# Context queries and keys kept on chip, and five reorderings, in a two-layer mixer step on one core

## The chip, the cores and the metric

The kernel is one program on one core of a Trainium2 chip. Its engines are TensorE (PE: matrix products and, through products with an identity, transposes), VectorE (DVE), ScalarE (ACT), GpSimd (POOL) and SyncE (SP, which here only issues DMAs). Each runs its own list of instructions in order, and they meet through semaphores. The metric is the time of one execution on the device in microseconds (us); lower is better.

## The reference

256 context tokens (`prompt`) and 1024 latent tokens (`sample`), each of 1024 numbers, pass two layers, all in float32.

```python
h = rmsnorm(x, norm1) * (1 + sc1) + sh1            # sc1, sh1: columns of silu(cond) @ w_mod + b_mod
# layer 0
proj = h @ w_in                                    # c_q 384 | c_kv 256 | k_rope 32 | gate_b, gate_c, u: 512 each
q = rmsnorm(rmsnorm(c_q) @ w_q_up)                 # 8 heads of 96
k, v = mla_expand_kv(rmsnorm(c_kv), k_rope)        # 8 heads of 96 and 64
# latent tokens: q and k rotated; cached context keys (256) go ahead of their own keys (1024)
attn = softmax(q k / sqrt(96)) v                   # context tokens see context tokens only
conv = gate_b * short_conv(gate_c * u)             # 3 taps along the tokens, each group by itself
x = x + g1 * (concat(attn, conv) @ w_o)
# layer 1 mixes by a 2-D DFT and a linear map instead
# both layers end with 16 experts; each takes its best 32 context and 128 latent tokens
ye = (silu(xe @ w_gate) * (xe @ w_up)) @ w_down * g
x = x + g2 * zeros.at[idx].add(ye)
```

## The kernel before, in words

The work is cut into stages; each stage (`Stage`) has its own tiles and semaphores and ends with a barrier of all engines. In order: `projections`, `attention`, `output_and_choice` (tiles `mix`), `experts` of layer 0, `fourier_and_choice`, `experts` of layer 1. The token axis is cut into ten tiles of 128: tiles 0 and 1 are the context, tiles 2 to 9 the latent tokens. Two more tiles hold the cached context, of which only keys and values are made.

**Projections.** Before the tiles come the modulation vectors: eight products of `cond` with 1 MB loads of `w_mod` (`mod.step`, L216), added to the bias by DVE (L232), turned to columns by PE (L224) and used by DVE to scale and shift the normalised, transposed tile (L706, L709). SP issues the eight `w_mod` loads (four staging buffers, so that loads 4 to 7 wait for products 0 to 3), then the first columns of `w_in`, then the four small loads of the bias (L192), then the other weights. POOL issues the tiles of `x` (L459). PE then goes through each tile: latents (`latent_product`, L507), u part (L514), transposes of the previous tile's queries and keys (`query_turns`, `key_turns`, L491), transposes of this tile's latents (L483), c part (L514), query and key/value products (L539, L548), transposes of the tile after next (L469), b part (L514). Tiles 3 and 5 also make the values of the cached tiles in between the two halves of the b part, and the tile after each (4 and 6) turns the cached keys (`k_c`) right behind its own. DVE copies turned keys from PSUM to `k_out` (`keys_kept`, L728), of which there is one buffer, and SP stores it to HBM (`kt`); `q_out` goes to `qt` likewise. For the convolution DVE writes `gated` = gate_c x u, applies three taps into `conv_o` (L747, L751), multiplies by gate_b (L755), and SP stores each half to `conv`.

**Attention.** SP loads the context's queries and keys from `qt` and `kt` (L905, L906), then values, the first latent queries, and ten pieces of the latent tokens' keys (L916). PE works through 72 slots (one head of one tile, for the context one head of both tiles): scores (L965 context, L980 latent), transposes, values. The output weights `w_o` are loaded during the last tile's slots into a tile `room` that outlives the stage.

**Output (`mix`).** SP loads attention and convolution rows of the first tile (`mixed(0)`, L1400 and L1401), and PE multiplies them by `w_o` (L1462).

**Experts.** POOL gathers token rows by index and, behind each expert, adds its result to rows of HBM by a DMA that accumulates: `scatter_sample` (L1722, 128 rows) and `scatter_prompt` (L1729, 32 rows). A scatter waits for the landing of the one before it of its own kind, since rows may repeat. The context results of experts 12 to 15 come in one product, so four context scatters stand at the end.

Of the kernel before, what the change touches and what calls it, by code (L numbers as in the profile page):

```python
# [32 lines left out]
P = 128  # L33
# [227 lines left out]
def projections(nc, t, per):  # L261
# [10 lines left out]
    PAD = 1  # L272
    WIDTH = TOK + 4 * PAD
    with Stage(nc, "proj") as s:
# [23 lines left out]
        gated = s.sb("gated", [P, CJ, WIDTH])  # L298
# [11 lines left out]
        gated_flat = gated[:].rearrange("p j n -> p (j n)")  # L310
        w_mod = [gated_flat[:, 0:2 * D], gated_flat[:, 2 * D:4 * D], gate_b[:].rearrange("p a j n -> p (a j n)"),
                 h_t[1][:].rearrange("p k n -> p (k n)")]
# [27 lines left out]
        for n in range(NT):  # L340
            count(lp_uses, ("lat", n))
            if n == 0:
                count(tp_uses, ("x", 1))
            else:
                count(tp_uses, ("q", n - 1))
                count(tp_uses, ("k", n - 1))
            if n - 1 in CACHED_AT:
                count(tp_uses, ("k", NT + CACHED_AT[n - 1]))
            count(tp_uses, ("lat", n))
# [14 lines left out]

        def at(p):

            return PAD + p * PAIR + (2 * PAD if p else 0)

# [9 lines left out]
        with nc.Block() as block:  # L378

            @block.sync  # L380
            def _(sp):
# [10 lines left out]
                mod.load_bias(sp, 0)  # L392
# [22 lines left out]
                def queries_store(n):  # L415
                    for b in range(2):
# [3 lines left out]
                def keys_store(n):  # L420
                    for b in range(2):
# [3 lines left out]
                def conv_store(p, half):  # L425
                    sp.wait_ge(mixed, mix_uses[p, half] + 1)
                    j = slice(half * JH, (half + 1) * JH)
                    sp.dma_start(t["conv"].rearrange("j p n -> p j n")[:, j, p * PAIR:(p + 1) * PAIR], conv_o[:, j, :]).then_inc(conv_out[half], 16)
# [22 lines left out]
                for done, value in ((q_stored, 16 * NT), (k_stored, 16 * KEYT), (v_stored, 16 * KEYT), (lat_stored, 32 * PT),  # L451
# [4 lines left out]
            def _(pool):  # L456
                for n in range(NT):
# [4 lines left out]
            def _(pe):  # L462
# [102 lines left out]
                for n in range(NT):  # L565
# [10 lines left out]
                    if n - 1 in CACHED_AT:  # L576
                        key_turns(NT + CACHED_AT[n - 1])
# [3 lines left out]
                    if n < LAST:  # L581
                        c_part(n)
                    if n == 0:
# [20 lines left out]
            def _(act):  # L604
# [42 lines left out]
                def queries_kept(n):  # L647
                    wait(act, q_stored, 16 * n)
# [1896 lines left out]
```

## Time and profile before

| | |
|---|---|
| median of 3 runs | 2297.88 us (2296.34 to 2303.9) |
| profiled execution | 2297.82 us, of which the span of the profile is 2295.4 us |
| mean granted TensorE clock | 0.939 of full speed |
| PE busy | 89% of the span |
| DVE, ACT, POOL busy | 38%, 20%, 7% |
| HBM traffic | 403.98 MB, mean 176 GB/s |

All times in what follows are us from the start of the span. A timeline row gives the start, the duration of a run of equal instructions, the engine, the line, output<-inputs, the count, and in brackets how long the engine had been idle before and what ended that. "Idle before" is what a change can win back, and only on the engine that sets the end of its stage; in most stages that is PE.

### The profile page before, as it was taken

The page shows a single profiled execution, that of the slowest core. Times are in us where ns is not written, and L with a number is a line of the kernel's source. Part 1 is how long each engine was busy: PE and PEld are TensorE (multiplying, and loading weights), DVE is VectorE, ACT ScalarE, POOL GpSimd, SP SyncE. Part 2 cuts the span into 40 slices and gives each one's busy share as a digit, 9 for nine tenths or more (in the row PEclk, how much of TensorE's full clock was granted, in tenths as well). Part 3 has the DMA queues.
Part 4 walks back from the last instruction along what each step waited for, and adds up shares of the span by engine and source line. Part 5 has one row for each costly group of instructions (what it writes and reads, how often), then busy time and mean ns, then how long its engine had stood idle before and what let it go on. Part 6 is the DMA issues. An engine that isn't in the chain of part 4 may idle for free. (4 is left out here: it accounts for less than half of the span.)

```text
span 2295.4 us, 27522 instructions
## 1 busy us (share of the span) xinstructions
PE 2038.8 (89%) x11435; PEld 1433.3 (62%) x11435; DVE 862.9 (38%) x1791; ACT 469.3 (20%) x922; POOL 154.4 (7%) x134
## 2 busy tenths in 40 slices
PE   4999989959999998992999999976997199999996
PEld 2777767745666664441878787851443187878784
DVE  1354345345666563337222222215254722222221
ACT  1222222126665662111000000004122100000000
POOL 0000000000000000000011121111010001211111
PEclk8999999979999999995899999986998599999998
DMA  9211110058444224952568787816020766878771
GB/s 356 84 46 37 53 35 33 24 131 264 178 164 182 106 84 144 368 189 98 194 225 310 264 305 267 288 28 235 19 110 37 291 238 226 307 266 302 266 258 28
DMA packets 160981, 403.98 MB, mean 176 GB/s; under 512 B 12357, under 2 KB 31740, under 8 KB 154714
## 3 DMA queue, kind: packets, MB, share of 16 engines
q1 hardware_dynamic: 145322, 347.18, 42.2%
q0 software_dynamic: 15536, 55.06, 8.7%
q8 instruction: 90, 1.47, 0.3%
q14 instruction: 33, 0.27, 0.0%
HBM read 338.65 MB, written 63.55 MB: 175 GB/s over the span
## 5 line engine op out<-in xcount | busy, mean ns | idle before, releaser
L1776 PE MATMUL experts_gu<-experts_h_t,weights_w_gate 128*128 128x160 f32 x2048 | 303.7, 302 | 4.1 <-issue 4.1
L1776 PEld LDWEIGHTS experts_gu<-experts_h_t,weights_w_gate 128*128 128x128 f32 x2048 | 289.7, 192 | 19.2 <-issue 19.2
L1776 PE MATMUL experts_gu<-experts_h_t,weights_w_up 128*128 128x160 f32 x2048 | 300.2, 300 | 0.0
L1776 PEld LDWEIGHTS experts_gu<-experts_h_t,weights_w_up 128*128 128x128 f32 x2048 | 286.5, 191 | 0.0
L1800 PE MATMUL experts_dn<-weights_w_down,experts_hid 128*128 128x512 f32 x512 | 225.8, 594 | 0.0
L1841 DVE TENSOR_TENSOR experts_hid<-experts_act,experts_gu 128x160 f32<-128x160 f32 x128 | 41.1, 321 | 481.3 <-ACT experts_act L1830 481.3
L514 PE MATMUL proj_cv<-proj_h_t,proj_w_in 128*128 128x256 f32 x960 | 216.0, 384 | 2.6 <-DVE proj_h_t L709 2.6
L1830 ACT ACTIVATE experts_act<-experts_gu 128x160 f32<-128x160 f32 x128 | 38.8, 303 | 834.1 <-PE experts_gu L1776 834.1
L514 PEld LDWEIGHTS proj_cv<-proj_h_t,proj_w_in 128*128 128x128 f32 x960 | 184.0, 193 | 29.9 <-issue 4.7
L1800 PEld LDWEIGHTS experts_dn<-weights_w_down,experts_hid 128*128 128x128 f32 x512 | 94.8, 190 | 113.8 <-issue 113.8
L980 PE MATMUL attn_sc<-attn_keys_s,attn_q_s 96*128 96x512 f32 (+1 forms) x384 | 154.9, 539 | 3.8 <-DVE attn_pr_t L1113 2.7
L1462 PE MATMUL mix_acc<-layer_room,weights_w_down 128*128 128x512 f32 x320 | 144.2, 603 | 9.3 <-DMA weights_w_down<-conv 9.3
L1095 DVE TENSOR_REDUCE attn_least<-attn_sc 128x1 f32<-128x512 f32 (+1 forms) x192 | 109.6, 599 | 102.1 <-PE attn_sc L980 102.1
L980 PEld LDWEIGHTS attn_sc<-attn_keys_s,attn_q_s 96*128 96x128 f32 x384 | 67.8, 190 | 91.3 <-issue 63.9
L1046 ACT ACTIVATE attn_pr<-attn_sc,attn_neg 128x1280 f32<-128x1280 f32 x64 | 85.0, 1327 | 128.3 <-DVE attn_neg L1097 128.3
L1462 PEld LDWEIGHTS mix_acc<-layer_room,weights_w_down 128*128 128x128 f32 x320 | 59.8, 193 | 78.8 <-issue 76.2
L1053 ACT ACTIVATE attn_pr<-attn_pr,attn_inv 128x512 f32<-128x512 f32 (+2 forms) x144 | 106.3, 785 | 3.9 <-DVE attn_inv L1103 3.9
L507 PE MATMUL proj_lp<-proj_w_in,proj_h_t 128*128 128x384 f32 (+1 forms) x320 | 93.7, 452 | 3.3 <-DVE proj_h_t L709 3.3
L2097 PE MATMUL mix_banks<-weights_w_down,weights_w_up 128*128 128x512 f32 (+2 forms) x96 | 58.5, 749 | 32.8 <-DMA weights_w_down<-w_f_folded 32.8
L1113 DVE COPY attn_pr_t<-attn_sc 128x512 f32<-128x512 f32 x128 | 82.5, 686 | 1.7 <-PE attn_sc L994 1.7
L507 PEld LDWEIGHTS proj_lp<-proj_w_in,proj_h_t 128*128 128x128 f32 x320 | 61.5, 193 | 33.5 <-issue 5.2
L994 PE MATMUL attn_sc<-all_ident,attn_pr 128*128 128x128 f32 x640 | 80.7, 273 | 0.1
(357 smaller groups left out, 2066.4 us busy)
## 6 DMA issues: line engine op xcount, KB each, us to landing
weights_w_gate<-w_gate_l SPq DMA_DIRECT2D x32, 2048.0 KB, 9.5
weights_w_up<-w_up_l SPq DMA_DIRECT2D x32, 2048.0 KB, 17.2
weights_w_down<-w_down_l SPq DMA_DIRECT2D x32, 2048.0 KB, 16.4
attn_w_mod<-w_mod_l SPq DMA_DIRECT2D x40, 1024.0 KB, 5.1
proj_w_in<-w_in_l SPq DMA_DIRECT2D x3, 2048.0 KB, 19.2
proj_x<-x POOLq DMA_DIRECT2D x10, 512.0 KB, 3.9
weights_w_down<-x SPq DMA_DIRECT2D x10, 512.0 KB, 5.1
kt<-proj_k_out SPq DMA_DIRECT2D x12, 384.0 KB, 3.0
```

What stands on the lines that cost most here:

```text
L507: last = pe.matmul(lp[:, base:base + hi - lo], h_t[n // 2 % 2][:, k, cols], w_in[:, k, lo:hi], start=(k == 0), stop=(k == KD - 1))
L514: last = pe.matmul(cv[bank][:, j * PAIR:(j + 1) * PAIR], w_in[:, k, base + j * P:base + (j + 1) * P], h_t[p % 2][:, k, :], start=(k == 0), ...
L980: pe.matmul(sc[b][:, lo:hi], q_s[tile % 2][:, h * P:(h + 1) * P], keys_s[:, h, lo:hi], start=True, stop=True).then_inc(s_full, 1)
L994: last = pe.transpose(sc[b][:, m * P:(m + 1) * P], pr[b][:, m * P:(m + 1) * P], per.ident[:])
L1046: act.activation(pr[b][:], sc[b][:, 0:K], ACT.Exp, bias=neg[b][:, 0:1], scale=-1.0, accum_out=total[b][:, 0:1]).then_inc(p_ready, 1)
L1053: act.activation(pr[b][:, lo:hi], pr[b][:, lo:hi], ACT.Copy, scale=inv[b][:, a:a + 1]).then_inc(p_scaled, 1)
L1095: ch.add(dve.tensor_reduce(least[:, k:k + 1], sc[b][:, lo:hi], AX.X, ALU.min))
L1113: dve.tensor_copy(pr_t[n % 4][:, lo:hi], sc[n % 2][:, lo:hi]).then_inc(v_kept, 1)
L1462: last = pe.matmul(acc[u][:, half * BANK:(half + 1) * BANK], a_t[u][:, k, :], w_o[:, k, half * BANK:(half + 1) * BANK], start=(k == 0), st ...
L1776: last = pe.matmul(gu[j % 2][:, m * SLOTS:(m + 1) * SLOTS], w[u][:, k, j * P:(j + 1) * P], h_t[u][:, k, :], start=(k == 0), stop=(k == KD ...
L1800: last = pe.matmul(dn[half][:], hid[i][:, k, 0:CAP_S], wd[i][:, k, cols], start=(k == 0), stop=(k == KF - 1))
L2097: last = pe.matmul(out[0:dst.shape[0], cols], stationary, moving, start=(m == 0), stop=(m == len(terms) - 1))
```

## The change

Seven pieces, in the order of the program:

1. The four bias loads go from SP's queue to the head of POOL's, ahead of the tiles of `x`. The `w_mod` staging moves to other buffers (two of them in `room_a`).
2. PE turns the cached keys after the c part of tiles 4 and 6, and the cached latents ahead of the b part of tiles 3 and 5; DVE and ACT are reordered to match.
3. `gated` is kept per pair of tiles, with the two columns at its edges copied, and the last taps write to the region of `conv_o` whose store is older.
4. Queries and keys of tiles 0 and 1 are written into `room_a` (`room.q_p`, `room.keys_p`) and read there by the attention: four stores to and four loads from HBM vanish, with PE's waits for them.
5. The first `mixed` rows are loaded during the last slots of the attention (`load_first`); `w_o` is loaded in two halves.
6. At the end of each layer the last latent scatter is issued between the second and third of the four context scatters.
7. One more stage (`rest0`) holds what follows the projections in layer 0: one more barrier at the layer's end.

```diff
@@ projections, SP's list
                 sp.dma_start(w_in[:, :, 0:LAT], w_in_d[:, :, 0:LAT]).then_inc(w_lat_in, 16)
-                mod.load_bias(sp, 0)
@@ POOL's list
             def _(pool):
+                mod.load_bias(pool, 0)
                 for n in range(NT):
@@ PE's list
                         key_turns(n - 1)
-                    if n - 1 in CACHED_AT:
-                        key_turns(NT + CACHED_AT[n - 1])
                     latent_turns(n)
...
                     if n < LAST:
                         c_part(n)
+                    if n - 1 in CACHED_AT:
+                        key_turns(NT + CACHED_AT[n - 1])
...
                     if n in CACHED_AT:
+                        latent_turns(NT + CACHED_AT[n])
                         b_part(n, 0, 1)
-                        latent_turns(NT + CACHED_AT[n])
                         kv_up(NT + CACHED_AT[n])
@@ ACT's queries_kept
+                    dst = room.q_p[0:QK, n, :] if n < PT else q_out[:]
@@ DVE's keys_kept
+                        if n < PT:
+                            dst, src = room.keys_p[0:QK, 4 * b:4 * b + 4, n * P:(n + 1) * P], tp[b][0:QK, :].rearrange("c (h k) -> c h k", h=4)
@@ DVE's gate
+                    if p >= 2:
+                        ch.add(dve.tensor_copy(here[:, :, 0:1], before[:, :, PAIR:PAIR + 1]))
+                        ch.add(dve.tensor_copy(before[:, :, PAIR + 1:PAIR + 2], here[:, :, 1:2]))
+                    if p == PAIRS - 1:
+                        ch.add(dve.memset(here[:, :, PAIR + 1:PAIR + 2], 0.0))
+                    ch.settle()
+                def taps(p, half):
+                    use, out, src = mix_uses[p, half], region(p, half), gated[:, p % 2, half * JH:(half + 1) * JH, :]
+                    wait(dve, conv_out[use % 2], 16 * (use // 2))
...
                 def convolve(p, half):
-                    lo = at(p)
                     dve.wait_ge(b_kept, 2 * p + half + 1)
-                    wait(dve, conv_out[half], 16 * p)
...
@@ DVE's list
-                    if n - 1 in CACHED_AT:
-                        keys_kept(NT + CACHED_AT[n - 1])
                     if n < LAST:
                         gate(n)
                         if n >= 2:
+                            taps(n // 2 - 1, n % 2)
                             convolve(n // 2 - 1, n % 2)
...
+                    if n - 1 in CACHED_AT:
+                        keys_kept(NT + CACHED_AT[n - 1])
                     query_sums(n)
@@ attention
-                for n in range(PT):
-                    sp.dma_start(q_p[:, n, :], t["qt"][n * QK:(n + 1) * QK, :]).then_inc(qp_in, 16)
-                    sp.dma_start(keys_p[:, :, n * P:(n + 1) * P], t["kt"][n * QK:(n + 1) * QK, :].rearrange("c (h k) -> c h k", h=HEADS)).then_inc(kp_in, 16)
                 sp.dma_start(vals_p[:], t["v"][0:SEQ, :].rearrange("(m p) c -> p m c", p=P)).then_inc(vp_in, 16)
...
                     if n == SLOTS_N - HEADS:
                         room.load_output_weights(sp, t)
+                        sp.wait_ge(o_out[0], 48)
+                        room.load_first(sp, t)
...
-                        if n == 0:
-                            pe.wait_ge(qp_in, 16 * PT)
-                            pe.wait_ge(kp_in, 16 * PT)
@@ output_and_choice
-                mixed(0)
                 choice.load(sp)
...
                pe.wait_ge(room.w_o_in, 32)
+                pe.wait_ge(room.first_in, 32)
                 product(0, 0, 0, KD)
@@ experts, POOL's list
                     if e == NE - 1:
                         for m in range(NE - BATCH, NE):
+                            if m == NE - 2:
+                                scatter_sample(e)
                             scatter_prompt(m)
...
```

PE's list around tile 3's b part and the whole of tile 4 up to its query products is, in the kernel before (`lat_c`, `k_c` are the cached tile's latents and keys, `xh` the tile after next, `cv` the c, b and u parts):

```order
L469 MATMUL proj_tp<-all_ident,proj_xh 128x128 x8
L514 MATMUL proj_cv<-proj_h_t,proj_w_in 128x256 x8
L483 MATMUL proj_tp<-all_ident,proj_lat_c 128x128 x2
L548 MATMUL proj_lp<-proj_w_kv,proj_lat_t 128x512 x4
L514 MATMUL proj_cv<-proj_h_t,proj_w_in 128x256 x8
L507 MATMUL proj_lp<-proj_w_in,proj_h_t 128x384 x8
L507 MATMUL proj_lp<-proj_w_in,proj_h_t 128x288 x8
L514 MATMUL proj_cv<-proj_h_t,proj_w_in 128x256 x16
L491 MATMUL proj_tp<-all_ident,proj_q_n 96x128 x8
L491 MATMUL proj_tp<-all_ident,proj_k_n 96x128 x8
L491 MATMUL proj_tp<-all_ident,proj_k_c 96x128 x8
L483 MATMUL proj_tp<-all_ident,proj_lat 128x128 x5
```

And the same stretch of PE's list in the changed kernel (its line numbers are a few lower):

```order
L466 MATMUL proj_tp<-all_ident,proj_xh 128x128 x8
L480 MATMUL proj_tp<-all_ident,proj_lat_c 128x128 x2
L511 MATMUL proj_cv<-proj_h_t,proj_w_in 128x256 x8
L545 MATMUL proj_lp<-proj_w_kv,proj_lat_t 128x512 x4
L511 MATMUL proj_cv<-proj_h_t,proj_w_in 128x256 x8
L488 MATMUL proj_tp<-all_ident,proj_q_n 96x128 x8
L488 MATMUL proj_tp<-all_ident,proj_k_n 96x128 x8
L480 MATMUL proj_tp<-all_ident,proj_lat 128x128 x5
L511 MATMUL proj_cv<-proj_h_t,proj_w_in 128x256 x16
L488 MATMUL proj_tp<-all_ident,proj_k_c 96x128 x8
```

The cached latents moved from behind the first half of the b part to ahead of it, and the cached keys from directly behind the tile's own keys to behind the tile's c part.

POOL's list ends, in the kernel before (L1717 gathers, L1722 is the latent scatter, L1729 the context scatter), with:

```order
L1722 DMA y_sample<-experts_ys,all_at_s 1024x1024
L1717 DMA experts_xs<-xh_sample,all_at_s 128x1024
L1729 DMA y_prompt<-experts_yp,all_at_p 256x1024
L1722 DMA y_sample<-experts_ys,all_at_s 1024x1024
L1729 DMA y_prompt<-experts_yp,all_at_p 256x1024 x4
L1722 DMA y_sample<-experts_ys,all_at_s 1024x1024
```

and in the changed kernel with:

```order
L1759 DMA y_sample<-experts_ys,all_at_s 1024x1024
L1766 DMA y_prompt<-experts_yp,all_at_p 256x1024
L1759 DMA y_sample<-experts_ys,all_at_s 1024x1024
L1766 DMA y_prompt<-experts_yp,all_at_p 256x1024 x2
L1759 DMA y_sample<-experts_ys,all_at_s 1024x1024
L1766 DMA y_prompt<-experts_yp,all_at_p 256x1024 x2
```

Of the four context scatters two now stand behind the last latent scatter; layer 0 ends with the same rows on its own tensors.

## Rows read from the trace of the kernel before

**Rows 1.** Waits of PE by line and releaser: total us, times, longest.
```profile
PE proj_tp L483 <- DVE proj_k_out L728: 10.1, 9, 3.4
...
PE proj_lp L548 <- ACT proj_lat_t L623: 2.3, 2, 1.2
```

**Rows 2.** Timeline of all engines, 0 to 60 us.
```profile
3.57 1.32 POOL L459 DMA_DIRECT2D proj_x<-x  x2 [3.12 <-POOLq L2440]
...
7.66 1.06 ACT L610 ACTIVATE proj_junk<-proj_x 128x1024 f32<-128x1024 f32 x1 [0.26 <-DMA proj_x<-x]
...
11.46 1.97 PE L469 MATMUL proj_tp<-all_ident,proj_xh 128*128 128x128 f32 x8 [4.28 <-DVE proj_xh L699]
...
15.27 1.19 SPq L181 DMA_DIRECT2D proj_gated<-w_mod_l  x2
...
21.98 5.06 SPq L192 DMA_DIRECT2D proj_mod_bias<-b_mod_l  x4
...
37.29 0.69 DVE L232 TENSOR_TENSOR proj_mod_rows<-proj_up,proj_mod_bias 128x512 f32<-128x512 f32 x1 [15.85 <-DMA proj_mod_bias<-b_mod_l]
...
42.49 10.89 PE L507 MATMUL proj_lp<-proj_w_in,proj_h_t 128*128 128x384 f32 x32 [3.34 <-DVE proj_h_t L709]
```

**Rows 3.** Tile proj_x, 2 to 70 us: issue to landing.
```profile
DMA to landing us min/median/max: 4.0/7.3/8.1
```

**Rows 4.** Windows: length, busy by engine, PE clock, DMA share, GB/s.
```profile
6.00:36.00 30.00, 13.68 (x75) 2.98 (x75) 1.27 (x4) 4.36 (x8) 0.53 (x1) 0.82 1.02 419
```

**Rows 5.** Windows of one tile each: tile 2, tile 4, tile 6.
```profile
127.85:169.45 41.60, 40.70 (x178) 31.05 (x177) 18.55 (x41) 9.22 (x22) 0.53 (x1) 1.00 0.14 45
...
216.10:263.78 47.68, 43.54 (x187) 33.02 (x185) 19.50 (x40) 9.40 (x23) 0.53 (x1) 0.96 0.15 47
...
310.43:359.27 48.84, 44.22 (x186) 33.72 (x185) 19.48 (x40) 9.41 (x23) 0.00 (x0) 0.93 0.11 36
```

**Rows 6.** Timeline of all engines, tile 4.
```profile
235.04 1.15 PE L491 MATMUL proj_tp<-all_ident,proj_k_c 128*96 128x128 f32 x8 [0.50 <-DVE proj_k_out L728]
...
238.59 1.28 DVE L728 COPY proj_k_out<-proj_tp 96x512 f32<-96x512 f32 x2 [3.10 <-DMA kt<-proj_k_out]
```

**Rows 7.** Timeline of all engines, 484 to 500 us.
```profile
486.17 0.61 DVE L747 TENSOR_SCALAR proj_conv_o<-proj_gated,proj_conv_w 128x256 f32<-128x256 f32 x2 [2.25 <-DMA conv<-proj_conv_o]
...
494.94 0.32 SPq L905 DMA_DIRECT2D attn_q_p<-qt  x1
```

**Rows 8.** Timeline of PE, 500 to 545 us.
```profile
504.93 3.75 PE L965 MATMUL attn_sc<-attn_keys_p,attn_q_p 96*128 96x256 f32 x8 [19.19 <-DMA attn_keys_p<-kt]
...
533.29 2.67 PE L980 MATMUL attn_sc<-attn_keys_s,attn_q_s 96*128 96x512 f32 x6
```

**Rows 9.** Tile attn_keys_s: its loads (duration ns min/median/max, first and last start) and landing.
```profile
L916 SPq DMA_DIRECT2D attn_keys_s<-kt x10: 562/1622/4797, 498.5 to 517.4; - x10
...
DMA to landing us min/median/max: 7.6/8.3/12.5
```

**Rows 10.** Windows: the start of the attention.
```profile
489.50:520.00 30.50, 11.71 (x34) 8.00 (x36) 7.66 (x16) 7.97 (x23) 0.00 (x0) 0.50 0.96 208
```

**Rows 11.** Timeline of all engines, 870 to 890 us.
```profile
877.53 0.33 SPq L1400 DMA_DIRECT2D weights_w_down<-attn  x1
...
881.38 9.11 PE L1462 MATMUL mix_acc<-layer_room,weights_w_down 128*128 128x512 f32 x16 [7.61 <-DMA weights_w_down<-conv]
```

**Rows 12.** Timeline of all engines, 2262 to 2296 us.
```profile
2274.72 0.75 DVE L1875 SCALAR_TENSOR_TENSOR experts_ys<-experts_dn,all_g_s,experts_gate 128x512 f32<-128x512 f32 x1 [2.68 <-PE experts_dn L1800]
2277.29 1.32 POOL L1729 DMA_INDIRECT y_prompt<-experts_yp,all_at_p  x1 [3.02 <-DMA y_prompt<-experts_yp,all_at_p]
...
2283.23 1.55 POOL L1722 DMA_INDIRECT y_sample<-experts_ys,all_at_s  x1 [0.30 <-issue]
```

**Rows 13.** Windows: the last data of the span.
```profile
2288.00:2290.00 2.00, 0.00 (x0) 0.00 (x0) 0.00 (x0) 0.00 (x0) 0.00 (x0) 0.50 0.27 51
```

**Rows 14.** Waits of SP, 1540 to 1560 us: the three barriers at the end of layer 0.
```profile
SPq L133 <- PEq L133: 1.1, 3, 0.5
```

More of the change, by code:

```diff
@@ L271, in projections @@
     LAST = NT - 1
-    PAD = 1
-    WIDTH = TOK + 4 * PAD
     with Stage(nc, "proj") as s:
@@ L450, in _ @@
                 keys_store(LAST)
-                for done, value in ((q_stored, 16 * NT), (k_stored, 16 * KEYT), (v_stored, 16 * KEYT), (lat_stored, 32 * PT),
+                for done, value in ((q_stored, 16 * (NT - PT)), (k_stored, 16 * (KEYT - PT)), (v_stored, 16 * KEYT), (lat_stored, 32 * PT),
                                     (conv_out[0], 16 * PAIRS), (conv_out[1], 16 * PAIRS)):
@@ L739, in gate, with region @@
                     dve.wait_ge(c_kept, n + 1)
+                    if p >= 2:
[4 more added lines that the diff above has]
+                    ch.settle()
+                def region(p, half):
+                    return conv_o[:, (mix_uses[p, half] % 2) * JH:(mix_uses[p, half] % 2 + 1) * JH, :]
@@ L754, in convolve @@
-                    j = slice(half * JH, (half + 1) * JH)
-                    dve.tensor_tensor(conv_o[:, j, :], conv_o[:, j, :], gate_b[:, p % 2, j, :], ALU.mult).then_inc(mixed, 1)
+                    dve.tensor_tensor(region(p, half), region(p, half), gate_b[:, p % 2, half * JH:(half + 1) * JH, :], ALU.mult).then_inc(mixed, 1)
                 def sums(sq, ready_in, value, out, ready):
@@ L1462, in product @@
                         last = pe.matmul(acc[u][:, half * BANK:(half + 1) * BANK], a_t[u][:, k, :],
-                                         w_o[:, k, half * BANK:(half + 1) * BANK], start=(k == 0), stop=(k == KD - 1))
+                                         room.row(k)[:, half * BANK:(half + 1) * BANK], start=(k == 0), stop=(k == KD - 1))
                     if half == 1 and hi == KD:
@@ L1643, in experts @@
     with Stage(nc, f"experts{layer}") as s:
-        gate = room.room[:, 0:2, :] if room else s.sb("gate", [P, 2, D])
-        xs = [room.room[:, 6 + u, :] if room else s.sb(f"xs{u}", [P, D]) for u in range(2)]
-        xp = room.room[:, 5, :] if room else s.sb("xp", [P, D])
+        gate = room.parts[0][:, 0:2, :] if room else s.sb("gate", [P, 2, D])
+        xs = [room.row(6 + u) if room else s.sb(f"xs{u}", [P, D]) for u in range(2)]
+        xp = room.row(5) if room else s.sb("xp", [P, D])
         h_t = [s.sb(f"h_t{u}", [P, KD, SLOTS]) for u in range(2)]
@@ L1650, in experts @@
         hid = [s.sb(f"hid{b}", [P, KF, SLOTS]) for b in range(BATCH)]
-        ys = [room.room[:, 2 + u, :] if room else s.sb(f"ys{u}", [P, D]) for u in range(2)]
-        yp = room.room[:, 4, :] if room else s.sb("yp", [P, D])
+        ys = [room.row(2 + u) if room else s.sb(f"ys{u}", [P, D]) for u in range(2)]
+        yp = room.row(4) if room else s.sb("yp", [P, D])
         tp = [s.ps(f"tp{b}") for b in range(2)]
```

127 lines of the change are left out of this document (77 added, 50 removed).

## The prediction

> **What bounds the kernel now.** The page's busy shares come first: PE has 89% of the span, DVE 38%, the others less, so a change pays where PE stands idle, or at a stage's end where all engines wait for a transfer. The waits of PE, sorted by releaser, give the map. The one that reaches most places is that of the latents' transposes for a copy by DVE, nine times, longest 3.4 us [rows 1]. The timelines then show what each wait is for. At the start DVE idles 15.85 us for the bias and PE begins the first latents at 42.49 [rows 2]. A tile of the projections takes 41.60 us when nothing special happens, and 47.68 and 48.84 where cached keys are turned [rows 5]. The attention begins with 19.19 us of PE waiting for keys that this kernel itself stored [rows 8], the output stage with 7.61 us for its first rows [rows 11], and each layer ends with scatters behind an idle PE [rows 12]. The experts, the bulk of the span, are not touched except for that end.
>
> All sums are made against the profiled execution, 2297.82 us (2.4 us of it outside the span), which is within 0.1 us of the median of the three runs.
>
> **1. Bias on POOL's queue: 1.5 us (bounds -1.2 and 5.4).** The bias is issued at 21.98 behind everything that SP sent before it, and DVE uses it at 37.29; PE's first latents follow 5.2 us later [rows 2]. With the bias early, DVE could go on when PE's last modulation product is done, and the first latents wait for the first columns of `w_in`. From 6 to 36 us the DMA engines are full (share 1.02, 419 GB/s) [rows 4], and everything up to those columns is in that stretch, so they land at about 36 to 37. Were nothing else moved, PE could begin at about 37.1: a gain of 5.4.
>
> But POOL issues the tiles of `x` behind the bias now. Two `x` issues take 1.32 us, so four bias issues take 2.6; DVE must have zeroed the bias tile first, for which I allow 0.8. So `x` is issued at 3.57 + 3.4 = 7.0, when SP's loads are already in the queues. The first tile landed 4.1 us after its issue (7.66 less 3.57), later ones take 7.3 [rows 2, 3]. It then lands at 14.3 in place of 7.66, 6.6 later, and PE's transposes move from 11.46 to 18.1. PE's list has these ahead of the modulation products, and loads 4 to 7 wait for the products to free their buffers: the first goes from 15.27 to about 21.9. By then the first four have landed, the queues run empty, and 4 x 1.05 MB and 2.75 MB of `w_in` (1024 x 672 numbers) remain, 16.6 us at 419 GB/s, with some 2.5 us from an issue to data (4.1 less the 1.25 that half a megabyte takes). That is 41.0 in place of 42.49: 1.5. With SP's price for a bias issue (5.06 for four) and the longest landing, 8.1, `x` comes 3.3 us later still and the gain is about -1.2; both stay in the range.
>
> The Trainium skill ("DMA: Bandwidth & Descriptors", section "Issuing engines are not separate DMA queues") says that transfers started by different engines run on the same 16 DMA engines and interleave, and that issuing from several saves only the issue time. By that rule this piece gives nothing, and the total would be 1.5 us higher; the full DMA engines of [rows 4] agree with it, no run here has yet shown the order in which the bias would land.
>
> **2. Cached tiles: 10.5 us (8.0 to 11.5).** In tile 4 PE turns the cached keys at 235.04; DVE cannot copy them out before the store of the tile's own keys has landed, since there is one `k_out`: it waits 3.10 us for that DMA and copies from 238.59 [rows 6]; PE's next transposes need the same PSUM and wait for that copy [rows 1]. Behind the wait PE's clock also falls: the mean granted clock is 0.96 and 0.93 in tiles 4 and 6, and 1.00 in tile 2 [rows 5]. The change puts the c part between the two, 32 products of 128x256, which at the least take four times the 1.15 us of the eight small ones [rows 6], so the store (issued when the copy of the tile's own keys ends) has landed before the cached keys are turned. The tile then takes that of an ordinary one plus the turn itself, 1.15 less the overlap of about 0.15: 42.6. That is 5.1 and 6.2 us for the two. What is late next is DVE's copy of the cached keys (1.28), which must be done before the transposes of the tile after next need the PSUM; the query and value products in between hide it. Without that cover it costs 1.28 in each tile.
>
> The cached latents lose a little: they stand right behind the transposes of another tile, whose PSUM DVE frees by two multiplications with an addition between (0.69 each for 128x512, as in DVE's row of [rows 2]), 2.07 less the 0.5 that the first half is done earlier, so some 1.6 us of waiting twice. The waits for the copies that they replace are 2.3 us in two [rows 1]. Net -0.8, no more than -0.9. So 11.3 less 0.8; the lower bound adds the two uncovered copies.
>
> **3. Last taps: 1.85 us (0.2 to 2.25).** DVE waits 2.25 us for a store of `conv_o` before the last taps [rows 7], and the copy of the last keys, whose store ends the stage, is queued behind. The other region's store is long done. Of that go the edge copies, on DVE in the last `gate`: three operations that the trace doesn't have. From below they cost nothing, since DVE waits for PE there; from above three times 0.69 [rows 2]. They write one or two columns, so I take 0.4. In the other tiles DVE, with its low share, hides them.
>
> **4. Context queries and keys: 9.7 us (5.8 to 13).** The stage's first DMA is at 494.94 [rows 7], PE begins at 504.93 [rows 8]. With the operands in place it begins when it is through the barrier, some 0.3 after SP: 495.2, so 9.7 earlier. What is late next are the latent keys: PE first reads them at 533.29, 28.4 after its beginning [rows 8], which becomes 523.6 on the old scale. Their last load is issued at 517.4 and lands 8.3 later, at 525.7 [rows 9]: a slack of 7.6. Four loads of 393 KB go from ahead of them; the DMA engines are full there (share 0.96 at 208 GB/s) [rows 10], so 1.57 MB make them 7.5 us earlier. Slack 7.6 + 7.5 - 9.7 = 5.4; with the longest landing, 12.5, still 1.2. If they come earlier only by SP's four issues (two thirds of the 3.6 between 494.94 and 498.5, 2.4 [rows 7, 9]) and take 12.5, PE waits 3.9: the lower bound 5.8. PE's clock is 0.50 in this stretch, with 11.71 us of products [rows 10]; if it rises some 6 us of products sooner, 3 more: the upper bound. The context's copies to the new places are as long as the old ones, on the same engines.
>
> **5. First rows of the output stage: 3.65 us (3.0 to 3.85).** SP is through the barrier at 877.53, PE begins at 881.38 [rows 11]. With the rows loaded one tile earlier, PE begins some 0.2 behind SP: 3.65. The loads are issued during the last tile's 8 slots, tens of us ahead, and wait only for stores of tiles done long before. The second tile's rows move up in SP's list by two issues and have a whole tile's product to land under.
>
> **6. Last scatters: 2.5 us in each layer, 5.0 (3.5 to 7).** Context scatters go out 4.3 us apart, since each waits for the one before (2277.29; the next ends 0.30 before 2283.23, so it began at 2281.60) [rows 12]. The latent scatter stands last, is ready when DVE ends at 2275.47, but is issued at 2283.23; data flows until about 2288.6 (a share of 0.27 in the last window) [rows 13]. Now it goes out at 2275.75 and takes POOL 1.55 us, to 2277.3, so the third context scatter starts at 2277.6, 0.3 late, and the fourth at 2281.9. That lands about 3.6 after its start (4.3 less the 0.7 until the next issue), at 2285.5; 0.5 MB of latent rows flow beside the third and may delay it by up to 1. The end moves from 2288.6 to 2285.5 to 2286.5: 2.1 to 3.1, I take 2.5, bounds 1.75 and 3.5. Layer 0 has the same list, and nothing of the next stage starts before the barrier, so twice.
>
> **7. One more barrier: -0.6 us (-0.4 to -2.3).** Three stand at the end of layer 0 already, with 1.1 us of waits in all [rows 14]; a fourth costs a third of that and some clearing, 0.6. At most: from the last data at 2288.6 to the end of the span, 2295.4, three stage ends take 6.8, so 2.3 for one.
>
> **Sum.** 1.5 + 10.5 + 1.85 + 9.7 + 3.65 + 5.0 - 0.6 = 31.6 us; 2297.82 - 31.6 = 2266.2, so 2266. All lower bounds together give 17.0 (2280.8), all upper 42.6 (2255.2).
>
> **The rivals.**
> - *The start gives nothing or loses* (the rule named above, or slow bias issues): the sum is 30.1 or 28.9, so 2267.7 to 2268.9. For it: `x` does queue behind the bias, and the DMA engines are full [rows 4]. Against: the first latents now wait for a bias that is last of all. 0.15.
> - *The latent keys become the bound of the attention's start.* Piece 4 falls to 5.8 at worst: 2270. For it: the slack rests on 1.57 MB fewer bytes ahead. Against: 5.4 us of slack by medians. 0.08.
> - *Tiles 4 and 6 find another wait*: DVE's new order (edge copies, taps, then the cached keys) is late for the next transposes and costs as much as the old wait in both, 2 x 3.2, so 2272.6. Against: DVE is 19.5 of 47.68 us busy in that tile [rows 5]. 0.08.
> - *PE's clock is better than before* in the attention's start: 2262 to 2255. 0.10.
> - *The change moves waits rather than removing them*: half of pieces 2, 4 and 5 comes back, 12 us, 2278. 0.05.
> - *Slower than before.* PE's clock stays at its lower level far into the attention, because PE works there from the start in short bursts between DVE and ACT. At the level of 0.50 [rows 10] products take twice as long, so each us there loses half a us: 63 us more at that level eat the 31.6, from 77 on the kernel is slower by more than 0.3%, and 90 would give 2311. Against: PE's gaps between the bursts are as long as before. 0.02, and 0.02 that the pieces cancel to no change.
>
> **How the numbers follow.** The forecast itself, 2261 to 2271 with the start at its middle value, has 0.50; the first rivals lie within 2267 to 2273. The range 2254 to 2280 reaches both sums of bounds. 0.3% of this kernel, 6.9 us, is about what a measurement can tell from no change; only the last rivals come near it. So faster 0.95, no change 0.03, slower 0.02.
>
> **What would show it.** First latents at about 41.0, bias ended long before DVE adds it; tiles 4 and 6 at 42.6 with a clock of 1.00 and no wait of DVE for a store of keys; no wait of PE at the attention's beginning, latent keys landed when PE comes to them; PE's first output product 0.2 us behind the barrier; the last context scatter at about 4.3 us behind the third, and 2.5 us less to the end of each layer. The prediction is wrong if the DMA engines at the start are idle longer than the bias saves, if the latent keys are waited for, or if DVE's new order shows up as waits of PE in every tile.

## The result: 28.5 us less, and where they came from

The changed kernel takes 2269.17 us (median of 4 runs, 2268.7 to 2275.16), the kernel before 2297.65 (median of 4): ratio 0.9877, 95% interval 0.9852 to 0.9901. Forecast were 2266 and a range of 2254 to 2280. The profiled execution took 2269.41 us, 2267.0 of it the span, 28.4 less than the span before.

A span hides which piece did what, so the two traces were cut at the same instructions. "First latents" is the start of the first latent product, "tile 0" from there to the next, "tiles 1 to 8" to the last latent product, "last tile" on to DVE's first zeroing in the attention, "attention" on to DVE's first in the output stage, "output" on to POOL's first gather, "experts 0" on to the first of the last four context scatters, "end 0" on to layer 1's first transfer by POOL, "layer 1" on to the first of its last four context scatters, "end 1" to the end of the span. All in us:

| stage | before | changed | difference | forecast of the pieces in it |
|---|---|---|---|---|
| first latents | 42.49 | 43.03 | +0.5 | -1.5 |
| tile 0 | 43.84 | 45.93 | +2.1 | 0 |
| tiles 1 to 8 | 355.27 | 344.32 | -10.95 | -10.5 |
| last tile | 53.52 | 51.47 | -2.05 | -1.85 |
| attention | 382.48 | 373.27 | -9.2 | -9.7 |
| output | 204.73 | 200.49 | -4.2 | -3.65 |
| experts 0 | 445.64 | 444.68 | -1.0 | 0 |
| end 0 | 27.06 | 25.13 | -1.9 | -2.5 + 0.6 |
| layer 1 | 713.68 | 714.72 | +1.0 | 0 |
| end 1 | 26.69 | 23.96 | -2.7 | -2.5 |

The timeline of the changed kernel's start, all engines, shows the piece that went the other way:

```profile
4.63 2.29 POOL L192 DMA_DIRECT2D proj_mod_bias<-b_mod_l  x4 [4.18 <-DVE proj_mod_bias L205]
...
6.92 1.09 POOL L456 DMA_DIRECT2D proj_x<-x  x2
15.91 1.06 ACT L607 ACTIVATE proj_junk<-proj_x 128x1024 f32<-128x1024 f32 x1 [9.65 <-DMA proj_x<-x]
...
19.71 1.97 PE L466 MATMUL proj_tp<-all_ident,proj_xh 128*128 128x128 f32 x8 [13.67 <-DVE proj_xh L698]
...
23.55 0.33 SPq L181 DMA_DIRECT2D proj_gate_b<-w_mod_l  x1
...
37.76 0.69 DVE L232 TENSOR_TENSOR proj_mod_rows<-proj_up,proj_mod_bias 128x512 f32<-128x512 f32 x1 [11.27 <-PE proj_up L216]
...
41.66 0.69 DVE L708 TENSOR_TENSOR proj_h_t<-proj_h_t,all_shift 128x512 f32<-128x512 f32 x1
...
43.03 11.43 PE L504 MATMUL proj_lp<-proj_w_in,proj_h_t 128*128 128x384 f32 x32 [3.87 <-DMA proj_w_in<-w_in_l]
```

`x` is issued at 6.92 and lands at 15.9, 9.0 us later, where the first tile took 4.1 before [rows 2]. Everything that hangs on it moves: PE's transposes to 19.71, the fifth weight load to 23.55. DVE no longer waits for the bias, but adds it at 37.76, no sooner than before, since the products are late; and PE now waits for `w_in` instead. That wait is last by only 0.7 us: DVE, late with the products, ends the scaled tile at 42.35 (41.66 and 0.69), as in the kernel before (42.34). So an earlier `w_in` alone would have given no more than that.

The windows of tiles 4 and 6 of the changed kernel (length, busy by engine, PE clock, DMA share, GB/s) answer to [rows 5]:

```profile
218.96:261.44 42.48, 41.58 (x187) 31.86 (x185) 19.26 (x42) 9.41 (x23) 0.53 (x1) 1.00 0.16 53
308.48:350.95 42.47, 41.57 (x186) 31.86 (x185) 19.26 (x42) 9.40 (x23) 0.00 (x0) 1.00 0.13 41
```

Both have the clock at 1.00 and 42.5 us. PE's timeline around the first of them shows why, and what tile 3 pays:

```profile
207.21 0.30 PE L480 MATMUL proj_tp<-all_ident,proj_lat_c 128*128 128x128 f32 x1 [0.44 <-DVE proj_h_t L705]
208.45 0.33 PE L480 MATMUL proj_tp<-all_ident,proj_lat_c 128*128 128x128 f32 x1 [0.94 <-DVE proj_h_t L705]
...
245.48 1.04 PE L488 MATMUL proj_tp<-all_ident,proj_k_c 128*96 128x128 f32 x8
```

The cached keys are turned without a wait; the cached latents wait twice for DVE, 1.4 us in all, where in the kernel before the key and value product behind them waited 1.16 for ACT's copy [rows 1].

DVE's timeline at the end of the last tile has the last taps without the wait of [rows 7]:

```profile
475.82 0.61 DVE L760 TENSOR_SCALAR proj_conv_o<-proj_gated,proj_conv_w 128x256 f32<-128x256 f32 x2
```

PE's timeline at the attention's beginning, for [rows 8]:

```profile
484.60 3.75 PE L980 MATMUL attn_sc<-layer_room_a 96*128 96x256 f32 x8 [7.18 <-PEq L133]
...
512.98 3.40 PE L995 MATMUL attn_sc<-attn_keys_s,attn_q_s 96*128 96x512 f32 x6
```

PE starts 0.04 us behind SP's first DMA (484.56), not 9.99. The latent keys, issued and landed by the view of their tile as

```profile
L932 SPq DMA_DIRECT2D attn_keys_s<-kt x10: 636/1510/2353, 485.5 to 498.2; - x10
...
DMA to landing us min/median/max: 6.2/7.9/8.6
```

are there at 506.8 at the latest, 6 us before PE reads them at 512.98.

One row each of DVE's and PE's timelines at the output stage's beginning, and POOL's timeline at the end of layer 1, answer to [rows 11, 12]:

```profile
858.02 0.06 DVE L1582 MEMSET mix_eps<- 128x1 f32 x1 [6.28 <-PEq L133]
...
858.14 6.16 PE L1498 MATMUL mix_acc<-layer_room_a,rest_first 128*128 128x512 f32 x8 [3.94 <-PEq L133]
```

```profile
2247.30 1.32 POOL L1766 DMA_INDIRECT y_prompt<-experts_yp,all_at_p  x1 [2.94 <-DMA y_prompt<-experts_yp,all_at_p]
2250.07 1.55 POOL L1759 DMA_INDIRECT y_sample<-experts_ys,all_at_s  x1 [1.46 <-DVE experts_ys L1915]
2251.93 1.32 POOL L1766 DMA_INDIRECT y_prompt<-experts_yp,all_at_p  x1 [0.30 <-issue]
2257.42 1.31 POOL L1766 DMA_INDIRECT y_prompt<-experts_yp,all_at_p  x1 [4.17 <-DMA y_prompt<-experts_yp,all_at_p]
```

PE begins 0.12 us behind DVE. The third context scatter starts 0.3 late, as forecast, and the fourth 5.49 behind it in place of 4.31.

### The profile page after: what moved, and what is told of

Read it like the earlier page. It is cut to its first block and busy times, and to the rows that moved or that the text cites. A ratio compares the mean times of both kernels' runs of the same rounds, so it can differ in the third digit from the quotient of the medians.

```text
span 2267.0 us, 27538 instructions
## 1 busy us (share of the span) xinstructions
PE 2036.6 (90%) x11435; PEld 1431.2 (63%) x11435; DVE 864.4 (38%) x1804; ACT 469.5 (21%) x922; POOL 155.8 (7%) x138
## 5 line engine op out<-in xcount | busy, mean ns | idle before, releaser
L1009 PEld LDWEIGHTS attn_sc<-all_ident,attn_pr 128*128 128x128 f32 x640 | 74.0, 141 | 6.8 <-ACT attn_pr L1068 0.5
L1030 PE MATMUL attn_o<-attn_pr_t,attn_vals_s 128*64 128x128 f32 x1280 | 76.9, 275 | 0.6 <-DVE attn_pr_t L1128 0.6
```

The lines of the kernel that those rows point to most:

```text
L1009: last = pe.transpose(sc[b][:, m * P:(m + 1) * P], pr[b][:, m * P:(m + 1) * P], per.ident[:])
L1030: last = pe.matmul(o_ps[VH * side:VH * (side + 1), base:base + width], vals[:, m, h * VH:(h + 1) * VH], pr_t[n % 4][:, m * width:(m + 1) * ...
```

## The experiments

Twelve runs. Five are the changed kernel with one piece undone (the bias, the cached tiles, the attention's operands, the first rows, the last scatters), three move one of its edits to another place, two put several such edits together, and two repeat the changed kernel and the kernel before. Pieces 3 and 7 have no run that undoes them alone. One execution of each was profiled; spans differ by several us in stages that no edit touches (layer 1 alone took 710.9 to 717.1 in the fourteen profiles), so each piece is priced in its own stage.

**The start.** Three places for the bias:

```diff
@@ bias_behind: back on SP
             def _(pool):
-                mod.load_bias(pool, 0)
...
                 sp.dma_start(w_in[:, :, 0:LAT], w_in_d[:, :, 0:LAT]).then_inc(w_lat_in, 16)
+                mod.load_bias(sp, 0)
@@ x_then_bias: on POOL behind two tiles of x
-                mod.load_bias(pool, 0)
                 for n in range(NT):
+                    if n == 2:
+                        mod.load_bias(pool, 0)
                     wait(pool, x_ready, n - 1)
@@ bias_head_sp: on SP ahead of the weights
-                mod.load_bias(pool, 0)
...
+                mod.load_bias(sp, 0)
                 for n in range(4):
                     mod.load(sp, n)
```

> The changed kernel with the bias loads back on SP behind the first columns of w_in; all else as changed. Theory 1 (x is late because it queues behind the bias and beside the weights): the first tile of x lands at about 7.7 us in place of 15.9, the first latents start at 42.5 in place of 43.0, tile 1's latents at 86.4 in place of 88.96, and the span is 2.6 us shorter, 2264.4. Theory 2 (the start is set by the bytes that must come before the first latents, and the place of the bias does not matter): first latents at 43.0, tile 1 at 89.0, span 2267.

Measured: 2267.41 us (4 runs, 0.9874 of before, 0.9854 to 0.9894). First latents at 42.71, near the 42.5 of theory 1, but tile 1's at 88.31, not 86.4: tile 0 still took 45.6. So the place of the bias does not explain tile 0. As to the start, 42.71 lies below the seven profiles with the bias in the changed kernel's place (42.75 to 44.52) by too little to decide; the next run does.

> The changed kernel with the bias on POOL's queue behind the first two tiles of x instead of ahead of them. Theory 1 (x late): x lands at about 7.7, PE's first transposes start at 11.5 in place of 19.7, the weight loads 4 to 7 start at 15.3 in place of 23.6, DVE adds the bias at about 31.5, the first columns of w_in land at about 36.5 and the first latents start at about 36.8; 6 us less at that point, of which the other weights of tile 0 may keep some: span 2259 to 2263. Theory 2 (bytes set the start): first latents at 42 to 43, span 2266 to 2267.

Measured: 2261.66 us (4 runs, 0.9843 of before, 0.9824 to 0.9862), first latents at 36.98. Its timeline, all engines (the rows to set beside the changed kernel's above):

```profile
4.78 2.03 POOL L192 DMA_DIRECT2D proj_mod_bias<-b_mod_l  x4
...
7.51 1.06 ACT L608 ACTIVATE proj_junk<-proj_x 128x1024 f32<-128x1024 f32 x1 [0.42 <-DMA proj_x<-x]
...
11.31 1.97 PE L467 MATMUL proj_tp<-all_ident,proj_xh 128*128 128x128 f32 x8 [4.43 <-DVE proj_xh L699]
...
31.17 0.69 DVE L232 TENSOR_TENSOR proj_mod_rows<-proj_up,proj_mod_bias 128x512 f32<-128x512 f32 x1 [9.68 <-PE proj_up L216]
```

The same four loads, one row lower in POOL's list: `x` lands at 7.5, DVE adds the bias 6.6 us earlier than in the changed kernel, and only `w_in` is waited for (PE 4.41 us). Theory 2 fell. Of the 6.05 us at the first latents 5.07 are left at tile 1's (83.89), since tile 0 took 46.9.

> The changed kernel with the bias ahead of the weight loads on SP's queue, so that POOL starts with x. Theory 1 (x late): x lands by about 9, PE's first transposes start at about 12 to 13; the weights start one bias later (2.3 to 5 us), and the first latents at 38 to 41. Theory 2 (bytes set the start): 42 to 43. Theory 3 (an early bias itself is what delays whatever follows it, on any queue): the weights are late by 8 as x was, first latents after 44.

Measured: 2262.28 us, first latents at 38.24, `x` landed by 7.92, the four bias issues 1.14 us at the head of SP's list. Theory 1 again. The first latents are 1.26 us later than with the bias behind `x`, about the 1.14 us of issues: an early bias by itself costs little more than its issues.

**The cached tiles.** Both moves undone on PE, ACT and DVE (`key_turns` and `keys_kept` of the cached tile back behind the tile's own, `latent_turns` back behind `b_part(n, 0, 1)`, `latents_kept` behind `key_root`).

> The changed kernel with the cached keys and latents at their old places on PE, ACT and DVE; all else as changed. Theory 1 (the one buffer k_out and its store made the wait, and the clock fell behind it): tiles 4 and 6 take 47.7 and 48.8 us again in place of 42.5, tiles 3 and 5 46.65 in place of 47.0, DVE waits 3.1 and 3.2 us for the store of keys, the clock in tiles 4 and 6 is below 1.00, and the span is 10.9 us longer, 2277.9. Theory 2 (the shorter chain of the convolution made the tiles shorter): tiles 4 and 6 stay within 1 us of 42.5.

Measured: 2277.51 us. Windows of tiles 4 and 6, then DVE in tile 4:

```profile
217.94:265.59 47.65, 43.54 (x186) 32.98 (x185) 19.73 (x42) 9.41 (x23) 0.53 (x1) 0.96 0.15 47
312.24:361.06 48.82, 44.67 (x186) 34.07 (x185) 19.73 (x42) 9.41 (x23) 0.00 (x0) 0.93 0.11 36
```

```profile
240.40 1.29 DVE L730 COPY proj_k_out<-proj_tp 96x512 f32<-96x512 f32 x2 [3.07 <-DMA kt<-proj_k_out]
```

Times, clocks and the wait for the store are all back, and tiles 1 to 8 take 355.05: 10.7 more. The span, 2275.7, is only 8.7 longer, since other stages were shorter in this execution (tile 0 took 44.07). Theory 1; the convolution's chain has no part in it.

**The attention's first operands**, by way of HBM again into the same tiles (abridged):

```diff
 def keys_store(n):
-    if n < PT:
-        return
...
+for n in range(PT):
+    sp.dma_start(q_p[:, n, :], t["qt"][n * QK:(n + 1) * QK, :]).then_inc(qp_in, 16)
+    sp.dma_start(keys_p[:, :, n * P:(n + 1) * P], ...).then_inc(kp_in, 16)
...
+pe.wait_ge(qp_in, 16 * PT); pe.wait_ge(kp_in, 16 * PT)
```

> The changed kernel with the context's queries and keys stored to HBM and loaded again at the attention's start, into the same tiles; all else as changed. Theory 1 (PE waited for these loads alone): PE's first scores come about 10 us behind SP's first DMA of the stage in place of 0.04, the latent keys are issued some 2.5 us later and still land before PE needs them, and the span is 9.2 to 9.9 us longer, 2276.2 to 2277. Theory 2 (the loads also hold the latent keys, which matter by themselves): PE waits at its first latent scores, and the span is more than 11 us longer.

Measured: 2273.09 us, a span of 2271.0, only 4 more. But the stage, from DVE's first to the next stage's, takes 381.78 in place of 373.27, 8.5 more, and PE begins 8.4 behind SP (483.04):

```profile
491.42 3.75 PE L980 MATMUL attn_sc<-layer_room_a 96*128 96x256 f32 x8 [15.55 <-DMA layer_room_a<-kt]
```

The rest is in stages that the edit doesn't touch: this execution had a tile 0 of 44.09 and a layer 1 of 712.22. Theory 1, a little smaller; theory 2 fell, PE has no wait at its first latent scores (519.81). `queries_store` is changed as `keys_store` is.

**The output stage's first rows** at its own head again (`room.load_first` moved from the last tile's slots to where `mixed(0)` stood).

> The changed kernel with the first rows of the output stage loaded at the head of that stage again, into the same tile; all else as changed. Theory 1: PE's first product starts 3.7 us behind the barrier, and the second tile's rows are waited for 1.7 us again, since they stand two issues later in SP's list: span 3.2 + 1.1 = 4.3 us longer, 2271.3. Theory 2 (the second tile's wait comes from elsewhere, and PE's clock, low at that point either way, gives some back): 2.5 to 3.3 us longer, 2269.5 to 2270.3.

Measured: 2269.15 us. PE's first product starts 3.9 us behind DVE (862.51 and 858.61) in place of 0.12, and its next operation on the router 19.31 behind DVE in place of 16.51: 2.8, and the stage takes 203.13 in place of 200.49. The span does not show it: at 2266.4 it is 0.6 shorter than the changed kernel's, as layer 1 took 710.85 in this execution and 714.72 in that one. By its stage, theory 2: eight products of the first tile take 5.17 in place of 6.16, the clock gives back 1.0. The later wait of 1.70 for rows, which the kernel before had, is 0.65 in the changed kernel and 0.50 here, so it is not this piece's.

**The last scatters**: the latent one behind all four, as before, and one place later than in the change.

```diff
@@ scatters_back
-                            if m == NE - 2:
-                                scatter_sample(e)
                             scatter_prompt(m)
+                        scatter_sample(e)
@@ scatter_later
-                            if m == NE - 2:
+                            if m == NE - 1:
                                 scatter_sample(e)
```

> The changed kernel with the last latent scatter behind all four context scatters; all else as changed. Theory 1 (the last latent scatter was issued late for no reason): the context scatters are 4.3 us apart to the last, data ends about 5.4 us behind the issue of the latent one, and each layer's end is 2.3 to 2.8 us later; span 2271.6 to 2272.6. Theory 2 (the gain of the ends came from elsewhere, the barrier or the next stage): within 1 us of 2267.

Measured: 2275.24 us; ends 27.38 and 26.5 in place of 25.13 and 23.96, 2.25 and 2.5 more (theory 1). The rest of the 6.4 by which the span is longer lies in stages that the edit doesn't touch.

> The changed kernel with the last latent scatter between the third and the last context scatter, one place later. In the changed kernel the last context scatter starts 5.49 us behind the third in place of 4.31. Theory 1 (the latent rows' data flow beside the third context scatter and delay its landing by 1.2 us, and would delay the last one the same way): the last starts 4.3 behind the third, lands 1.2 late, and the end of each layer is about 0.3 us earlier: span 2266.0 to 2266.8. Theory 2 (what delayed the third was POOL's work on the latent scatter right before it, and data beside it cost nothing): each layer's end is 1.2 to 1.5 us earlier: 2264.0 to 2264.6.

Measured: 2265.49 us; ends 24.07 and 23.28, 1.06 and 0.68 less than in the changed kernel. POOL's timeline at the end of layer 1:

```profile
2248.84 1.31 POOL L1766 DMA_INDIRECT y_prompt<-experts_yp,all_at_p  x1 [3.02 <-DMA y_prompt<-experts_yp,all_at_p]
2250.45 1.55 POOL L1759 DMA_INDIRECT y_sample<-experts_ys,all_at_s  x1 [0.31 <-issue]
2253.11 1.32 POOL L1766 DMA_INDIRECT y_prompt<-experts_yp,all_at_p  x1 [1.11 <-DMA y_prompt<-experts_yp,all_at_p]
```

The last starts 4.27 behind the third, as both theories say. From there to the end of the span it is 10.29 us (2263.4 less 2253.11), in the changed kernel 9.58 (2267.0 less 2257.42): 0.7 more. The view of its landings says the same: the last context scatter landed 4.1 us after its start, and 3.5 in the changed kernel, where nothing flows beside it. So the latent rows do cost a neighbour something, 0.6 to 0.7 here where theory 1 has 1.2 and theory 2 nothing, and the gain of each end lies between the two (0.3, and 1.2 to 1.5). The span, 2263.4, is below both, through stages that the edit doesn't touch.

**Together** (`best`). Four edits: the bias behind two tiles of `x`, the latent scatter one place later, the cached latents (not the keys) at their old place, and `room.extend` without a stage of its own, so without the added barrier.

> Four edits on the changed kernel: the bias behind the first two tiles of x on POOL's queue; the last latent scatter one place later; the cached latents at their old place on PE and ACT (their keys stay behind the c part); no extra stage, so one barrier less in layer 0. From the stages of the runs so far: first latents at 37.0 in place of 43.0 and tile 1 at 83.9 in place of 89.0; tiles 3 and 5 46.65 in place of 47.0; the ends of the layers 24.07 and 23.28 us behind the last context result, and 0.3 to 0.6 less of it in layer 0 without the barrier. Together 5.1 + 0.7 + 1.6 + 0.5 = 7.9 us less than the changed kernel, about 2261. Rival: the start is all that counts, 5 us, about 2264.

Measured: 2258.34 us (5 runs), 0.9837 of before (0.9815 to 0.9859). First latents at 37.32, tile 1's at 81.05; tiles 3 and 5 46.6 in place of 47.0; ends 23.30 and 22.93. Layer 0's end is 0.8 less than in the experiment before, which has the barrier; layer 1's, which is the same in both, is 0.35 less too. The span is 10.6 less than the changed kernel's where 7.9 were expected; 2.2 of it are tile 0 (43.73), which no edit was meant to touch. All five runs lie below the rival's 2264.

**One more edit** on that kernel (`best_turns`):

```diff
                     for base, lo, hi in ((0, 0, QL), (BANK, QL, LAT)):
+                        if n == 0 and base:
+                            x_turns(1)
...
                     if n == 0:
-                        x_turns(1)
                         pe.wait_ge(w_part_in[2], 16)
```

> The kernel of the run before with one more edit: PE turns the second tile of x between the two parts of the first latents in place of behind them. Theory 1 (PE is idle 2.56 us there because the u part of a pair waits for DVE to scale and shift its second tile, and the clock granted after that gap is lower, so that the u part takes 8.6 to 8.8 us in place of 7.1): the gap goes and the u part takes 7.1, together up to 4 us less, tile 1's latents at about 80 in place of 83.9. Theory 2 (the lower clock in the u part has nothing to do with the gap): 2.5 us less, tile 1's latents at about 81.4 and a u part of over 8 us, or the same loss in another place of tile 0.

Measured: 2255.57 us (5 runs), 0.9818 of before (0.9801 to 0.9835), tile 1's latents at 79.69, 1.36 less than in `best`. PE's timeline shows the u part:

```profile
50.14 7.17 PE L514 MATMUL proj_cv<-proj_h_t,proj_w_in 128*128 128x256 f32 x32 [0.38 <-DMA proj_w_in<-w_in_l]
```

The gap ahead of it falls from 2.56 to 0.38, and it takes 7.17. But `best` has the whole gap and a u part of 7.14, so the gap alone does not cost what theory 1 says. Against `best` itself the gain is about what runs differ by.

**Both kernels once more**, unedited.

> The changed kernel once more, unedited, for what a stage varies by itself. Theory 1 (the 2.1 us that tile 0 takes longer than in the kernel before come from the clock granted there in this execution and not from an edit): with first latents at 42.7 to 44.5 as in the experiments, tile 0 may take 44 or 46 us, and layer 1 from its first transfer to its last context result anything from 711 to 715. Theory 2 (the edit at the start costs them): tile 0 takes 45.6 to 46.5 again, as in most of the experiments with the bias early.

> The kernel before once more, unedited. Theory 1 (the clock of tile 0 is not the change's doing): tile 0 takes 43.8 or 45.6 to 46.5, and the attention 381 to 383 us from its first DMA to the next stage. Theory 2: 43.8 again, the u part 7.1.

Measured: 2268.8 and 2298.2 us. Tile 0 takes 45.98 in the changed kernel and 43.66 in the kernel before, each within 0.2 of its first profile, while first latents (44.40 after 43.03), the attention before (380.32 after 382.48) and layer 1 (712.12 after 714.72; 716.98 after 713.68) move by 1.4 to 3.3. Both times of tile 0 are those of theory 2, and theory 1 has no support as put. Yet the cause that theory 2 names falls too: with the bias early and `x` late, two experiments (cached tiles back, keys by HBM) had 44.1, and with the bias behind, one had 45.6.

## Why the prediction was right, point by point

The forecast of 2266 was 3.2 us too low, and the range and the sign held. By the table, piece 1 accounts for 2.0 of the 3.2 and tile 0 for 2.1; all other stages together came out 0.9 better than forecast. Part of that closeness is luck: layer 1 alone took 710.9 to 717.1 us in the fourteen profiles, and in these two it differed by only 1.0, made up by experts 0. By its steps:

- **Piece 1 failed**: a gain of 1.5 us was forecast, and the first latents came 0.5 later (1.9 in the second pair of profiles). The mechanism was forecast in full (`x` behind the bias, PE's transposes, the freed buffers, `w_in` last); mis-sized was the landing of `x`, put at 7.3 and measured at 9.0, which moved the transposes to 19.71 and not 18.1, and the fifth weight load to 23.55 and not 21.9. That is 1.6 us. Another 0.35 is a slip in the sum: 4.1 less 1.25 is 2.85 us from an issue to data, and not 2.5. With both the 41.0 forecast becomes 43.0, which is what was measured. The lower bound has a slip too: 3.3 us later makes a gain of 1.5 one of -1.8, not -1.2; and all lower bounds together, 2280.8, lie outside the range that is said to reach them. The rival that the start gives nothing or loses, at 0.15, came true, but for neither of the reasons that it gave: the bias issues were not slow (2.29 us for 2.6), and the place of the bias is not without effect.
- The Trainium skill ("DMA: Bandwidth & Descriptors", section "Issuing engines are not separate DMA queues") says that transfers started by any engine run on the same 16 DMA engines. The trace agrees: `x`, issued on POOL behind 4 MB of weights on SP, took 9.0 us, with the DMA engines full (share 1.02 from 6.92 to 15.91 us). What the prediction took from that section, that the place of the bias gives nothing, does not hold for this kernel: behind two tiles of `x` in POOL's list the first latents start 6 us earlier.
- **Tile 0** was not forecast at all: 2.1 us more. The u part took 8.53 us at a mean clock of 0.82 in the changed kernel, and 6.98 at 1.00 in `best`, 32 products each, as these windows show, one of each kernel:

```profile
57.89:66.42 8.53, 8.53 (x33) 7.21 (x33) 1.90 (x5) 0.00 (x0) 0.53 (x1) 0.82 1.04 404
```

```profile
51.53:58.51 6.98, 6.98 (x32) 6.11 (x33) 1.90 (x5) 0.00 (x0) 0.53 (x1) 1.00 1.03 406
```

- That is 1.55 of the 2.1; the first latents' own products are the rest (11.43 us against 10.89). The place of the bias does not decide it: tile 0 took 45.6 with the bias behind, and 46.9 with it behind two tiles of `x`. But the fourteen profiles show what goes with the loss. The first latents begin at the lower level of the clock (1.2 GHz, a granted clock of 0.50), and in thirteen profiles PE then has the 2.56 us gap ahead of the u part. In five of these the clock rose to its upper level (2.4 GHz) 3.0 to 3.75 us after the first latents' start, and the u part took 7.14 or 7.15 us. In the other eight it rose 4.0 to 6.0 us after it, fell again within 0.6 us of the gap's end, and the u part took 8.6 to 8.8. In `best_turns`, without the gap, it rose at 4.75 and did not fall. So the loss goes with a gap and a late rise together; no run changes the rise alone, and what sets its moment stays open.
- **Piece 2**: tiles 4 and 6 gave 5.2 and 6.4 (5.1 and 6.2 forecast), tiles 3 and 5 cost 0.3 and 0.4 (0.8 together forecast). Right, and shown by undoing it. DVE's new order hid the copy: in the changed kernel DVE never waits for a store of keys. The two moves are separate: `best`, with the latents at their old place, has 46.6 in tiles 3 and 5 and still 42.5 in tiles 4 and 6.
- **Piece 3**: 2.05 for 1.85. The edge copies took 0.3 us and not 0.4. No run undoes this piece; the last tile took 51.5 us in all twelve profiles that have it, and 53.5 in the two that don't.
- **Piece 4**: PE began 9.95 earlier in its stage (9.7 forecast), and the latent keys had at least 6 us to spare (5.4 forecast by the median landing, 1.2 by the longest). The stage kept 9.2 of it: the first latent scores took 3.40 us in place of 2.67 [rows 8]. Undoing it cost 8.5. In the second pair of profiles the stage is only 7.0 shorter (373.32 after 380.32); of the 2.2 by which the kernel before was faster there, 1.0 is that PE began 8.99 behind SP and not 9.99.
- **Piece 5**: 3.66 at PE's first product, 3.2 at the end of the first tile: with the wait went a part of what the clock had recovered. Undoing it cost 2.8. The output stage's other 1.05 is a wait of 1.70 that became 0.65; no edit was found to be its cause.
- **Pieces 6 and 7**: with the extra barrier 1.9 in layer 0, and 2.7 in layer 1, for 2.5 less 0.6 and 2.5. Undoing piece 6 shows 2.25 and 2.5. With it undone the end of layer 0 is 27.38, 0.3 above the kernel before's 27.06, which leaves about that for the barrier; leaving the barrier out gave 0.4 (`best_turns`) to 0.8 (`best`), with ends that vary by 0.2 to 0.4 without an edit. The third context scatter landed 1.2 late beside the latent rows (4.7 us after its start, 3.5 alone), for which up to 1 had been allowed, and the last one started that much later.
- Experts 0 and layer 1, which no edit reaches, moved by -1.0 and +1.0.

## What to carry to other kernels

When a small early transfer is pulled ahead, put it behind what the same queue's first consumer needs, not ahead: ahead of two tiles of `x` the same four loads made the first latents start 6 us later than behind them. In this kernel a wait for the store of a single output buffer could be filled with the next long product, without a second buffer. And price an edit in its own stage, between the same instructions of two traces: the span of a single execution moved by more than most of these edits, through stages that none of them touched.

## What was not expected of the hardware

- 0.5 MB issued on POOL behind 4 MB of weights on SP landed 9.0 us after its issue; as the first large load it took 4.1 [rows 2].
- Four bias issues took SP 5.06 us behind its other loads [rows 2], 1.14 at the head of its list, and POOL 2.0 to 2.3.
- An accumulating scatter of 32 rows landed 3.5 us after its start by itself, 4.7 when it started 1.86 us behind one of 128 rows, and 4.1 when it started 2.66 us behind it.
- The same 32 products at the same place of the program took 7.0 or 8.5 us, by the granted clock (1.00 or a mean of 0.82), with the same 2.56 us of idle time ahead of them.
